# Sixteen of the 24 input projection tiles of layer one as a one-level Strassen product in fp16 pairs

## What is computed

```python
def even_layer(x, norm_g, w_in, pool_w, pool_scale, conv_w, w_out):
    h = rms_norm(x, norm_g)
    proj = h @ w_in                    # (1024 x 1024) @ (1024 x 3072)
    u_a, z_a, h_b, b_b, c_b, z_b = jnp.split(proj, ...)     # six parts of 512 columns
    y_a = pool_mixer(u_a, pool_w, pool_scale) * jax.nn.silu(z_a)
    y_b = short_conv_mixer(h_b, b_b, c_b, conv_w) * jax.nn.silu(z_b)
    return x + jnp.concatenate([y_a, y_b], axis=-1) @ w_out
```

## Time and profile before

| | us |
|---|---|
| median of three runs | 1040.92 |
| lowest, highest | 1040.21, 1041.97 |
| the profiled execution | 1040.06 |
| its span | 1038.3 |

### The profile page before, as it was taken

How to read it: one execution, slowest core, us unless ns; L and a number is a source line. 1 busy time by engine, 2 the same in 40 slices (tenths; PEclk the granted TensorE clock), 3 DMA queues, 4 the chain that set the end, 5 groups by cost and what they waited for, 6 DMA issues and landing times.

```text
span 1038.3 us, 15500 instructions
## 1 busy us (share of the span) xinstructions
PE 1011.0 (97%) x5979; PEld 840.4 (81%) x5979; DVE 619.6 (60%) x1125; ACT 465.4 (45%) x882; POOL 212.3 (20%) x302
## 2 busy tenths in 40 slices
PE   5999999999999999999999999999999999999998
PEld 4888888888888888888888999997877777777887
DVE  5653554445643453311434599998999999997311
ACT  6311111111132322331234676767999888888000
POOL 0000000000000001110001286876863333231000
PEclk9999999999999999999999999999999999999999
DMA  9300111111333441321111153677587654530221
GB/s 283 50 27 21 51 51 41 56 46 41 106 114 125 145 150 51 108 60 42 41 41 39 58 193 141 204 193 202 104 205 163 125 121 103 103 103 2 102 92 71
DMA packets 166137, 103.10 MB, mean 99 GB/s; under 512 B 76208, under 2 KB 150448, under 8 KB 165808
## 3 DMA queue, kind: packets, MB, share of 16 engines
q1 hardware_dynamic: 158992, 101.73, 35.0%
q10 hardware_dynamic: 7072, 0.39, 0.6%
HBM read 55.96 MB, written 29.36 MB: 82 GB/s over the span
## 4 chain that ended last, share of the span: by engine, by line
PE 76%; DVE 11%; ACT 5%; issue 3%; POOL 3%; DMA 1%; SPq 0%; DVEq 0%; POOLq 0%; ACTq 0%
PE banks L106 23%; PE banks L108 23%; PE banks L107 23%; PE banks L1639 4%; ACT heads_probs_big L1319 2%; PE banks L1657 2%; DVE heads_probs_big L1451 1%; ACT heads_pt_hi L1328 1%; DVE heads_y L1442 1%; POOL heads_prod L1553 1%; DVE heads_x L1437 1%; DVE heads_x L1438 1%; PE banks L1658 1%; DVE heads_ss L1484 1%; DMA front_w<-in_w_in_ab 1%
## 5 line engine op out<-in xcount | busy, mean ns | idle before, releaser
L106 PE MATMUL banks<-front_act_hi,front_w_hi 128*128 128x512 f32 x608 | 239.7, 394 | 10.9 <-DVE front_w_lo L526 10.9
L108 PE MATMUL banks<-front_act_hi,front_w_lo 128*128 128x512 f32 x608 | 237.8, 391 | 0.0
L107 PE MATMUL banks<-front_act_lo,front_w_hi 128*128 128x512 f32 x608 | 237.8, 391 | 0.0
L106 PEld LDWEIGHTS banks<-front_act_hi,front_w_hi 128*128 128x128 f32 x608 | 114.9, 189 | 36.8 <-issue 8.5
L107 PEld LDWEIGHTS banks<-front_act_lo,front_w_hi 128*128 128x128 f32 x608 | 114.9, 189 | 24.2 <-issue 0.5
L108 PEld LDWEIGHTS banks<-front_act_hi,front_w_lo 128*128 128x128 f32 x608 | 114.8, 189 | 24.1
L1459 DVE TENSOR_TENSOR heads_pt_lo<-banks,heads_pt_hi 128x512 f16<-128x512 f32 (+2 forms) x192 | 102.1, 554 | 16.5 <-ACT heads_pt_hi L1328 12.1
L393 ACT ACTIVATE front_w_hi<-front_w 128x1024 fp32r<-128x1024 f32 x43 | 45.6, 1060 | 147.2 <-DMA front_w<-in_w_in_ab 102.7
L375 POOL TENSOR_TENSOR front_sq<-front_sq,front_squares 128x1024 f32<-128x1024 f32 x6 | 14.4, 2398 | 450.3 <-ACT front_squares L488 450.3
L1328 ACT ACTIVATE heads_pt_hi<-banks 128x512 f16<-128x512 f32 (+2 forms) x192 | 88.6, 484 | 11.0 <-PE banks L1639 10.8
L530 DVE TENSOR_TENSOR front_w_lo<-front_w,front_w_hi 128x1024 fp32r<-128x1024 f32 x43 | 52.4, 1220 | 42.9 <-ACT front_w_hi L393 42.6
(11 more groups left out here) (265 smaller groups left out, 2065.1 us busy)
## 6 DMA issues: line engine op xcount, KB each, us to landing
qk_scratch<-heads_y SPq DMA_DIRECT2D x22, 512.0 KB, 3.8
front_w<-in_w_in_ab SPq DMA_DIRECT2D x21, 512.0 KB, 3.8
front_w<-in_w_in_c SPq DMA_DIRECT2D x17, 512.0 KB, 4.0
qk_scratch<-heads_last_y SPq DMA_DIRECT2D x10, 512.0 KB, 3.7
y<-in_x_t SPq DMA_DIRECT2D x8, 512.0 KB, 8.1
front_w<-in_w_out_ab SPq DMA_DIRECT2D x8, 512.0 KB, 3.7
front_x<-in_x_t SPq DMA_DIRECT2D x8, 512.0 KB, 5.1
x_scratch<-front_x SPq DMA_DIRECT2D x8, 512.0 KB, 3.9
```

What stands on the lines that cost most here:

```text
L106: nc.tensor.matmul(out, w_hi, a_hi, start=first, stop=False)
L107: nc.tensor.matmul(out, w_hi, a_lo, start=False, stop=False)
L108: return nc.tensor.matmul(out, w_lo, a_hi, start=False, stop=last)
```

## The change

**Gates first.** The four `z_a` and four `z_b` tiles keep the old form and become tiles 0 to 7 (`MIX_TILES` is 8 now). They go straight to `y`, where SiLU is applied in place.

**Pairs.** The other 16 tiles become eight pairs (`PAIRED`): of each group first `u` with `hb`, then `bb` with `cb`. A pair is a 256x1024 by 1024x1024 product, cut in halves along output channels, input channels and tokens, and done by seven products (`FORMS`) of 128x512 outputs over 4 slices (`CHUNKS`) in three passes: 84 matmuls with fp16 operands.

**Right-hand sides, once.** `first_forms(c)`, for c = 0 to 3, scales two rows of `x` by gamma and `rstd_all` (L821), splits the first half of one and all of the other into fp16 pairs, and has GpSimd form four combinations of 128x512 (`t1` to `t4`), of which `t1` is split here too. c = 0 stands ahead of the evacuation of tile 0, c = 1 behind it, c = 2 and 3 behind the evacuations of tiles 2 and 3. `later_forms()` splits the other twelve pieces when tile 7 has finished.

**Left-hand sides, for every pair.** VectorE takes the largest weight (`pair_peak`, a reduction of 128x2048), TensorE sums it over partitions (`row_sum`, one 128x1 matmul), VectorE makes a scale (`pair_scale`, three small ones), GpSimd four sums of 128x512, ScalarE seven fp16 casts (`pair_forms`) and VectorE seven remainders (`pair_low`).

**Outputs.** Three banks serve a pair, five of the seven products share two of them. After products 0, 1 and 2 ScalarE copies a bank away (`snapshot`), and product i + 2 adds to that bank; for i = 2, 3, 4 `pair_product` waits for the copy. VectorE writes three quarters (`quarter`, after products 3, 4 and 5), ScalarE the last one. Product 6 waits for the second quarter of its own pair. `pool_sums` and `map_low` now stand in the odd pairs, the output and the convolution of the previous group in the even ones; one tap of the convolution has moved to ScalarE (`first_tap`).

**After the pairs.** The first two output tiles are interleaved, six slices of each, then the last two (`first_out_tiles`).

```diff
-        for n in range(RING, OUT0 + 2):
+        sp.dma_start(gam_row[:], gamma.unsqueeze(0).to_broadcast([P, D])).then_inc(gam_row_in, 16)
+        for n in range(RING, OUT0):
             load(n)
+        for p in range(RING):
+            load_pair(p)
...
+        for c in range(CHUNKS):                       # GpSimd
+            pool.wait_ge(h_ready, 2 * c + 2)
+            if c:
+                pool.wait_ge(act_low, 3 * c)
+            nc.gpsimd.tensor_tensor(t1[:], low[:, halves[1]], low[:, halves[0]], ALU.subtract).then_inc(t_added, 1)
...
+        def later_forms():                            # ScalarE
+            act.wait_ge(proj_ready, OUT0)
+            act.wait_ge(t_added, 4 * CHUNKS)
+            for n in range(3):
+                for c in range(CHUNKS):
+                    nc.scalar.activation(t_form[:, n, 0, c], t_raw[n][c][:], ACT.Copy).then_inc(act_high, 1)
...
+        def first_forms(c):                           # VectorE
+            if c:
+                dve.wait_ge(t_added, 4 * c)
+                dve.wait_ge(act_low, 3 * c)
...
+        def pair_product(p, i):                       # TensorE
+            pe.wait_ge(form_low, FORMS * p + i + 1)
+            if i in (2, 3, 4):
+                pe.wait_ge(snapped, 3 * p + i - 1)
+            if i == 6:
+                pe.wait_ge(c_done, 3 * p + 2)
...
+        def paired():
+            for p in range(PAIRED):
+                for i in range(FORMS):
+                    pair_product(p, i)
+                    if p + 1 < PAIRED and i == (1 if p else 4):
+                        row_sum(p + 1)
+                    if p % 2 and i == 5:
+                        pool_map(p // 2)
```

More of the change, by code:

```diff
@@ new lines, in scalar @@
+        act.dma_start(head_g[:, 0], q_head_g.to_broadcast([P, QKH])).then_inc(small, 16)
+        act.dma_start(head_g[:, 1], k_head_g.to_broadcast([P, QKH])).then_inc(small, 16)
+        spread_out(1)
+        first_forms(0)
+        act.wait_ge(small, SMALL)
+        def paired():
+            later_forms()
+            for p in range(PAIRED):
+                g = p // 2
+                snapshot(p, 0)
+                snapshot(p, 1)
+                if p and p % 2 == 0:
+                    first_tap(g - 1)
+                if p % 2:
+                    weight_map(g)
+                snapshot(p, 2)
+                if p == 1:
+                    high(OUT0)
+                if p + 1 < PAIRED:
+                    pair_forms(p + 1, range(FORMS))
+                else:
+                    for n in (1, 2):
+                        high(OUT0 + n)
+                    for i in range(3):
+                        y_split(i)
+                if p + 1 == PAIRED:
+                    for i in range(3, 6):
+                        y_split(i)
+                last_quarter(p)
+            y_split(6)
+            first_tap(GROUPS - 1)
+            y_split(7)
@@ new lines, in pair_low, with quarter @@
+        def pair_low(p, which):
+            for i in which:
+                dve.wait_ge(form_high, FORMS * p + i + 1)
+                nc.vector.scalar_tensor_tensor(form_split(p, i, 1), form(p, i), w_scale[:, p % 2:p % 2 + 1],
+                                               form_split(p, i, 0), ALU.mult, ALU.subtract).then_inc(form_low, 1)
+        def quarter(p, order):
+            done, shot, m, h = ((4, 2, 0, 1), (5, 1, 1, 1), (6, 0, 0, 0))[order]
+            dve.wait_ge(pair_ready, FORMS * p + done)
+            dve.wait_ge(snapped, 3 * p + shot + 1)
+            nc.vector.scalar_tensor_tensor(pair_dest(p, m)[:, halves[h]], pair_bank(p, done - 1),
+                                           unscale[:, p % 2:p % 2 + 1], snap[:, shot], ALU.mult, ALU.add).then_inc(c_done, 1)
```

484 lines of the change are left out of this document (373 added, 111 removed).

## The result

The changed kernel takes **1048.6 us** (median of four runs, 1048.0 to 1050.9), the kernel before beside it 1040.6: a ratio of 1.008, 95% interval 1.0061 to 1.0099. It is 8 us slower where I had forecast no change and a range up to 1047. The profiled execution has a span of 1046.3 (before 1038.3).

What follows compares the result with a forecast made beforehand. TensorE, busy 97% of the span, was taken as the bound. 26.3 us less work minus losses of 12.2, 1.7, 5.7, 4.9 and 1.2 left 0.6 gained: median 1040.3, no change, range of 8 in 10 from 1034 to 1047.

Steps and rivals of the forecast that it cites:

- TensorE's work: From 49.85 to the first output tile: 207.6 us of work against 233.9, so 26.3 us less.
- first chain (tiles 3, 4): Tiles 3 and 4 wait for VectorE's first_forms blocks, evacuations and tile 4's weight split: loss 12.2 us.
- clock: TensorE's clock drops after the idle time ahead of tiles 3 and 4, paid in tile 4: loss 1.7 us.
- pair 0: Waits counted from pair 0's first product, at product 2, the row sum and product 6: loss 5.7 us.
- pairs 1 to 7: Waits mainly at product 6 for the second quarter, and at pair 7's map: loss 4.9 us, range 0 to 12.
- restarts: First matmul after each of eleven TensorE waits takes 0.11 us longer: loss 1.2 us.
- The rival of 0.2267: The pairs' fp16 matmuls keep 0.2267 us each instead of 0.217: 3 us net slower, 1043.5; chance 0.13.
- the lock: VectorE and GpSimd exclude each other for whole instructions; first chain ends at 78.4, 5.4 us later; chance 0.17.
- The chain without any sharing: The first chain if GpSimd does not slow VectorE: ends at 71.0, loss 10.3 us.
- the faster rival: VectorE and GpSimd hardly disturb each other, clock holds, pairs 1 to 7 hardly wait: 1033.5 to 1037, say 1035.5; chance 0.25.
- What was free: Input scale, weight loads of pairs 1 and 2 and the convolution's tail after pair 7 were counted as costing nothing.
- VectorE becomes the bound: Rival in which whole-instruction exclusion lengthens each first_forms block by 1.6 us and slows the pairs: median 1048; chance 0.17.

Runs made afterwards that it cites:

- e1: The changed kernel with GpSimd's sixteen subtractions t1 to t4 left out, memsets in their place: 1038.3 us, ratio to the kernel before 0.9975.
- the probe: A program of its own in which VectorE repeats an instruction alone and beside GpSimd: eight two-SBUF-input subtractions took 4.90 us alone, 15.62 beside GpSimd's of 1024.
- e7: The changed kernel with GpSimd's four sums per pair (s1 to s4) left out for all eight pairs: 1045.7 us.
- e10: The changed kernel with e5's reorderings, further order changes, GpSimd's sums for pair 1 held back and tile 6's SiLU behind the third snapshot: 1020.0 us, ratio 0.9797.
- e5: The changed kernel with the first chain, pair 0 and quarters reordered together, splits for tiles 5 to 7 and the row sum moved: 1021.3 us; run again, 1023.2.
- e2: The changed kernel with tiles 0 to 2 evacuated before any first_forms block and tile 4's weights split early: 1042.0 us, ratio 1.0013.
- e4: The changed kernel with VectorE doing both first quarters ahead of the next pair's scale and first two remainders in pairs 1 to 6: 1046.1 us, ratio 1.0046.
- e6: The changed kernel with 26 unused matmuls added on TensorE before tile 3 and 32 before tile 4: 1048.9 us.
- e8: The e6 kernel with 45 instead of 32 unused matmuls before tile 4: 1047.0 us, ratio to the kernel before 1.0065.

## Why the prediction was wrong

TensorE's work from 49.85 to the first output tile, and what was lost there, in us:

| step | predicted | measured |
|---|---|---|
| TensorE's work | 207.6 | 207.0 |
| first chain (tiles 3, 4) | 12.2 | 16.8 |
| clock | 1.7 | 4.7 |
| pair 0 | 5.7 | 5.4 |
| pairs 1 to 7 | 4.9 | 6.8 |
| restarts (measured: what is left) | 1.2 | 1.0 |

The losses are 34.7 (241.7 from 49.85 to 291.55, less 207.0) instead of 25.7.

**TensorE's work: right.** The row of the attention gave the pace: the first product of pair 0 has 12 matmuls in 2.59 us, 0.216 each. The rival of 0.2267 is refuted.

**The first chain: right in kind, 4.6 short.** The failed step is "The remainders that meet GpSimd thus go at two thirds of their speed: a block takes about 6.9". In its place the two engines take turns by whole instructions (e1, the probe), and a block takes 8.2, the weight split 2.2 instead of 1.7. The row behind the step, 1.49 instead of 0.95, was read without its neighbour. This GpSimd instruction stood ahead of the two shown there:

```profile
596.74 1.05 POOL L1137 TENSOR_TENSOR heads_x<-heads_x,gain 128x256 f32<-128x256 f32 x1
```

VectorE's instruction began at 597.12, this one ended at 597.79, and 0.95 from there is 598.7; VectorE's ended at 598.6: the row fits taking turns. The chain that I had worked out for the lock ended at 78.4; it ended at 77.5. I gave it 0.17 and let that one row decide against it, where the blocks put subtractions of 1.2 us against remainders of 0.6, which no row of before shows. The point of decision was right: the blocks took 8.2, above 8. The chain without any sharing was a wrong sum: its own pieces (47.05, three blocks of 6.0, evacuations of 1.2 and 2.3, the split of 1.2) end at 69.8 and not at 71.0, and e1 measured 69.2. The forecast doesn't use it, but sharing was worth 3.2 us by its own terms and not 2, so the faster rival was put too near and e1's expectation too high.

**The clock: one stretch predicted, three paid.** This term is the other large miss, 1.7 instead of 4.7. Tile 4: seven pitches make 1.6 and took 3.1, 1.6. Pair 0 behind the 2.56: 35 pitches make 7.6 and took 9.0, 1.4. Pair 5 behind a wait of 2.00: twelve make 2.6, and took 4.3, 1.7. The size of one stretch was right; I had set the clock against the two long waits alone, where waits of 2.00 and 2.56 us had one behind them too. That the stretch in tile 3 is hidden was right.

**Pair 0: the sum right, its parts not.** Measured are 1.36 before product 0, 2.56 before product 2, 0.45 and 1.00. The 1.36 are missing in the prediction, which counts "from its first product": that product waits for the evacuation of tile 7. It gave ScalarE a head start, so that product 2 lost 2.56 instead of 4.35. The twelve remainders took 11.6 and not the 7.5 that the chain of casts implied, without harm. Product 3 ends at 14.75 by the prediction's own terms and not at 14.95, which makes its 0.6 before the row sum 0.4; 0.45 was measured.

**Pairs 1 to 7: the right place, 1.9 short.** Waits at product 6 are 0.22, 1.29, 0.50, 1.27, 2.00 and 0.72, and 0.84 at the map of pair 7. Pairs 2 and 4 were put 0.7 too low: `ch` took 1.89, as in a lock, and e7 takes 0.6 back in each. Pairs 1, 3 and 5 lie 0.2 to 0.3 above their figures, pair 6 0.1 above and pair 7 0.2 below.

**What was free stayed free.** The scale of the input, the loads of pairs 1 and 2 and the convolution's tail brought no wait: the output tiles run through.

**The rival in place.** "VectorE becomes the bound" at 1048 was the result within 0.6 us, with its mechanism (e1, the probe) and its chain, though part of its sum was chance: it left out 3 us of clock, and its chain was 0.9 too long. That the loss is one of order, not of the method, shows in e10: the same products end 28.7 us below the changed kernel and 2% below the one before.

## What to carry to other kernels

Before work moves to GpSimd, write down beside which VectorE instructions it will run: beside two SBUF inputs or a fast one-input form both take turns, beside a PSUM source, a reduction or a memset nothing is lost, and a wait that holds GpSimd back can pay: some 2 us here. A saving on TensorE counts only when the other engines' lists are put in order of due time: list for every TensorE wait the weight split, the evacuation and the snapshot that it needs and what stands ahead of each; one forgotten split cost 8.9 us. Count a wait on TensorE for itself and for a possible stretch at half rate behind it: here waits of 2.0 us and more often had one, at 1.4 to 2.8 us each.

## What the runs showed of the hardware

- VectorE and GpSimd, both with long lists, alternate instruction by instruction: pitch 1.68 for 0.61 and 1.23, and 2.76 for 0.61 and 2.40. So the fewer and shorter GpSimd's instructions, the less VectorE loses.
- A one-input fp32 `TENSOR_SCALAR` went from 0.36 to 1.41 us in step with GpSimd. In pair 5 of e5 a `COPY` of 128x2 elements took 1.11 us, and ended with the GpSimd instruction beside it; its neighbours of 128x1 and 128x4 took 0.15 and 0.17.
- The half-rate stretches, 1.4 to 1.7 us of loss each in the changed kernel and up to 2.8 in others (tile 4 of e7), came behind waits of 2.0 us and more, but not behind each: after the same wait of 2.56 in pair 0 one came in the changed kernel, e2, e4, e6 and e7, and not in e1 and e8. What decides it is open.
